# Keys and values of the given memory, projected beside the matrix memory instead of ahead of the cross-attention's queries

## The reference

```python
h = rmsnorm(x, norm_mix_g)
p = h @ w_in                      # queries, keys, values, gates of all branches
attn_out = sliding_window_attention(aq, ak, av, attn_sinks, slopes)
m_h = mlstm_chunkwise(mq, mk, mv, gif[..., :H], gif[..., H:])   # 4 heads of 128
x = x + concatenate([attn_out, sigmoid(mo) * m_h]) @ w_out

hm = rmsnorm(mem, norm_mem_g)     # mem: 256 rows of 1024, an input
kv = hm @ wkv                     # 1024 x 2048: keys, then values
q = rmsnorm(x, norm_xattn_g) @ wq
a = softmax(q k^T / 16)           # 4 heads of 256, 1024 x 256 scores each
x = x + (a v) @ wo
```

## Time and profile before

| what | value |
|---|---|
| time, median of 3 runs | 2593.92 us (2593.26 to 2597.9) |
| time of the profiled execution | 2593.7 us, its span 2591.9 |
| mean granted TensorE clock | 0.964 |
| TensorE busy (PE) | 2443.2 us, 94% of the span |
| VectorE busy (DVE) | 1407.1 us, 54% |
| ScalarE busy (ACT) | 932.0 us, 36% |
| GpSimd busy (POOL) | 78.3 us, 3% |

### The profile page before, as it was taken

How to read it: one execution, slowest core, us unless ns; L and a number is a source line. 1 busy time by engine, 2 the same in 40 slices (tenths; PEclk the granted TensorE clock), 3 DMA queues, 4 the chain that set the end, 5 groups by cost and what they waited for, 6 DMA issues and landing times.

```text
span 2591.9 us, 41445 instructions
## 1 busy us (share of the span) xinstructions
PE 2443.2 (94%) x17958; PEld 1969.8 (76%) x17958; DVE 1407.1 (54%) x2515; ACT 932.0 (36%) x1565; POOL 78.3 (3%) x61
## 2 busy tenths in 40 slices
PE   6999988999999999999999999899999996789879
PEld 5777756788888888888888888677777875577757
DVE  4584855655435555543555555563444455766653
ACT  3445432444333333422333423443232232334341
POOL 0000000000000000000000000020000001100000
PEclk9999977999999999999999999899999998799989
DMA  6453310434112333333333343333212312011043
GB/s 192 123 147 107 83 32 1 155 107 137 56 50 87 97 95 96 96 96 101 95 96 96 94 128 96 107 95 125 67 58 67 104 57 106 6 41 41 10 138 115
DMA packets 359310, 233.06 MB, mean 90 GB/s; under 512 B 9556, under 2 KB 332244, under 8 KB 359000
## 3 DMA queue, kind: packets, MB, share of 16 engines
q1 hardware_dynamic: 356392, 224.83, 29.0%
q10 hardware_dynamic: 2736, 5.57, 0.6%
HBM read 211.50 MB, written 18.87 MB: 89 GB/s over the span
## 4 chain that ended last, share of the span: by engine, by line
PE 87%; DVE 8%; ACT 2%; DMA 2%; issue 1%; POOL 0%; SPq 0%; ACTq 0%; DVEq 0%; POOLq 0%
PE PS L1325 21%; PE PS L1327 20%; PE PS L1326 20%; PE PS L1706 5%; PE PS L1311 3%; PE PS L1345 1%; PE PS L1347 1%; PE PS L1346 1%; PE PS L1624 1%; PE PS L1578 1%; PE PS L1553 1%; PE PS L1644 1%; PE PS L1609 1%; PE PS L1590 1%; DVE SR L1837 1%
## 5 line engine op out<-in xcount | busy, mean ns | idle before, releaser
L1325 PE MATMUL PS<-SR 128*128 128x512 f32 (+1 forms) x2400 | 955.9, 398 | 39.9 <-DVE SR L1837 35.0
L1326 PE MATMUL PS<-SR 128*128 128x512 f32 (+1 forms) x2400 | 933.7, 389 | 0.0
L1327 PE MATMUL PS<-SR 128*128 128x512 f32 (+1 forms) x2400 | 933.4, 389 | 0.0
L1837 DVE TENSOR_TENSOR SR<-SB,SR 128x1024 fp32r<-128x1024 f32 (+1 forms) x328 | 396.7, 1211 | 393.3 <-ACT SR L2523 392.9
L1325 PEld LDWEIGHTS PS<-SR 128*128 128x128 f32 x2400 | 452.8, 189 | 156.3 <-DVE SR L1837 36.4
L1327 PEld LDWEIGHTS PS<-SR 128*128 128x128 f32 x2400 | 452.7, 189 | 95.9
L1326 PEld LDWEIGHTS PS<-SR 128*128 128x128 f32 x2400 | 453.2, 189 | 89.6 <-issue 1.9
L2523 ACT ACTIVATE SR<-SB 128x1024 fp32r<-128x1024 f32 (+1 forms) x328 | 338.8, 1036 | 277.3 <-DMA SB<-in_w_down 102.7
L1706 PEld LDWEIGHTS PS<-SB 64*64 64x64 f32 x4096 | 128.3, 136 | 40.6 <-issue 20.9
L1706 PE MATMUL PS<-SB 64*64 64x64 f32 x4096 | 141.0, 222 | 12.4 <-DVE SB L2403 5.9
L1311 PE MATMUL PS<-SB 128*128 128x128 f32 (+2 forms) x688 | 107.7, 293 | 28.0 <-DVE SB L2285 15.0
(11 more groups left out here) (261 smaller groups left out, 2463.7 us busy)
## 6 DMA issues: line engine op xcount, KB each, us to landing
SB<-in_w_in SPq DMA_DIRECT2D x110, 512.0 KB, 4.0
SB<-in_w_up SPq DMA_DIRECT2D x88, 512.0 KB, 3.9
SB<-in_w_out SPq DMA_DIRECT2D x32, 512.0 KB, 4.5
SB<-in_w_down SPq DMA_DIRECT2D x32, 512.0 KB, 4.2
SB<-in_w_ada SPq DMA_DIRECT2D x12, 1024.0 KB, 6.3
asides<-SB SPq DMA_DIRECT2D x40, 256.0 KB, 3.5
SB<-in_wkv SPq DMA_DIRECT2D x16, 512.0 KB, 4.0
SB<-in_wq SPq DMA_DIRECT2D x16, 512.0 KB, 4.2
```

What stands on the lines that cost most here:

```text
L1325: pe.matmul(out, whi[:, k - k0, :], hi[k], start=(k == 0), stop=False)
L1326: pe.matmul(out, whi[:, k - k0, :], lo[k], start=False, stop=False)
L1327: i = pe.matmul(out, wlo[:, k - k0, :], hi[k], start=False, stop=(k == j.K - 1))
L1837: v.tensor_tensor(m.f32r(a, kn * cn), m.f32(a, kn * cn), m.f32r(a + 1024, kn * cn).bitcast(F32), SUB).then_inc(*on("split.v", p))
```

## The change

`mem` is loaded into X0 + 6144, a part of x's place, by a new step `mem_load` that stands at `mark("g")`, behind mv1, ahead of the load of the reset mask. Its norm is a side of the first flow behind the gates; kx, vx0 and vx1 are the last jobs of the first flow's main chain, and wait for the norm. Keys go to `kxs` in the second half of x's place, in-place of `mem`, values to two places `vxs`. `x_again` copies the keys by a DMA within SBUF (1 MB, `kmove`) to their final place, loads six of eight tiles of x's first half, copies a half of the values (0.5 MB, `vmove`), waits for `kmove`, and loads the rest of x. The jobs and units that read these places wait for the new semaphores instead of the old ones. `memory()` is gone.

```diff
-        self.memT = [work(28672 + 256 * k, 256) for k in range(8)]
-        self.qx, self.kx, self.vx = v3(work(16384, 8192), 8), v3(work(24576, 2048), 8), v3(work(26624, 2048), 2)
-        self.Pv2, self.PTv2 = [work(28672, 1024), work(29696, 1024)], [work(30720, 1024), work(31744, 1024)]
+        self.memT = [f32(X0 + 6144 + 256 * k, 256) for k in range(8)]
+        self.kxs, self.vxs = v3(f32(X0 + 6144, 2048), 8), [work(a, 1024) for a in (7168, 30752)]
+        self.qx, self.kx, self.vx = v3(work(16384, 8192), 8), v3(work(28672, 2048), 8), [work(a, 1024) for a in (31776, 30752)]
+        self.Pv2, self.PTv2 = [work(24576, 1024), work(25600, 1024)], [work(26624, 1024), work(27648, 1024)]
...
-        self.HM = self.parts(W0 + 30720, W0 + 28672, 256)
+        self.HM = self.parts(X0, X0 + 3072, 256)
...
         job(f"out{h}", d["w_out"], 0, 128, 8, m.MX[h], lambda k, h=h: [("mix.v", "lo", h, k)], "add", "gemm.v",
-            cut=4, dst=lambda t, h=h: m.xs[h][t], wait=lambda t, h=h: [(f"xr{h}", 0)], half=h)
+            cut=4, dst=lambda t, h=h: m.xs[h][t], wait=lambda t, h=h: [("xa0", 0), (f"xr{h}", 0)] if not h and t > 5 else [("xr1" if h else "xa0", 0)], half=h)
...
-    job("kx", d["wkv"], 0, 128, 8, m.HM, normed("mem"), "copy", "gemm.a", N=256, dst=lambda t: m.kx[:, t, :],
-        wait=UP("pe", "kv0"))
+    job("kx", d["wkv"], 0, 128, 8, m.HM, normed("mem"), "copy", "gemm.a", N=256, dst=lambda t: m.kxs[:, t, :],
+        wait=[("rms.v", "o", "mem", 7)])
...
-        "mem": Norm(m.memT, lambda k: [("mem", 0)], col("g_mem"), m.HM, st(273, 2), mldone, T=256),
+        "mem": Norm(m.memT, lambda k: [("mem", 0)], col("g_mem"), m.HM, st(273, 2),
+                    [("gates.pe", "t")], T=256),
...
-                        self.flagged("g", ("mark", "g"))),
+                        self.flagged("g", ("mark", "g"), ("mem_load",)),
+                        self.after("mem"), T("kx"), N("vx0"), N("vx1")),
...
-                  self.mlstm(0, 2), self.mlstm(1, 3))
+                  self.mlstm(0, 2), self.mlstm(1, 3),
+                  chain(self.after("gates"), self.rms("mem", self.room)))
...
-        self.flow(chain(T("out0"), self.after("parts"), T("out1"), self.flagged("kv0", ("mark", "kv0")), self.after("mem"),
-                        self.memory(), self.after("x0"), T("q0"), self.flagged("q0", ("mark", "q0")), self.after("x1"), T("q1"),
+        self.flow(chain(T("out0"), self.after("parts"), T("out1"), self.flagged("kv0", ("mark", "kv0")),
+                        self.opened_x(), self.after("x0"), T("q0"), self.flagged("q0", ("mark", "q0")), self.after("x1"), T("q1"),
...
+    def mem_load():
+        for e in S.upto("pe", "g"):
+            w.wait_ge(*e)
+        sp.dma_start(v3(m.f32(X0 + 6144, 2048), 8), d["memT"].rearrange("(k p) n -> p k n", p=128)).then_inc(*on("mem", 0, by=16))
+
     def x_again():
+
         mlstm_done()
-        for h in range(2):
-            sp.dma_start(m.XT[:, :, 512 * h:512 * h + 512],
-                         d["xT"][:, 512 * h:512 * h + 512].rearrange("(k p) n -> p k n", p=128)).then_inc(*on(f"xr{h}", 0, by=16))
-            if not h:
-                sp.dma_start(v3(m.work(28672, 2048), 8), d["memT"].rearrange("(k p) n -> p k n", p=128)).then_inc(
-                    *on("mem", 0, by=16))
+
+        def tokens(h, k0, k1):
+            return sp.dma_start(m.XT[:, k0:k1, 512 * h:512 * h + 512],
+                                d["xT"][128 * k0:128 * k1, 512 * h:512 * h + 512].rearrange("(k p) n -> p k n", p=128))
+        sp.dma_start(m.work(28672, 2048), m.f32(X0 + 6144, 2048)).then_inc(*on("kmove", 0, by=16))
+        tokens(0, 0, 6).then_inc(*on("xa0", 0, by=16))
+        sp.dma_start(m.vx[0], m.vxs[0]).then_inc(*on("vmove", 0, by=16))
+        w.wait_ge(*at("kmove", 0))
+        tokens(0, 6, 8).then_inc(*on("xr0", 0, by=16))
+        tokens(1, 0, 8).then_inc(*on("xr1", 0, by=16))
```

More of the change, by code:

```diff
@@ L907, in cross @@
             yield from self.after(("cs", n - 1))
-        yield from self.after("kv", f"q{n // 4}")
+        yield from self.after(f"q{n // 4}")
         yield from self.room((self.pairs, 1), (self.P, 1))
@@ L936, in crosses, with opened_x @@
             yield from self.cross(units.pop(0))
+    def opened_x(self):
+        for i in range(2):
+            self.P.give(i, ("upto", "pe", "kv0"))
+            self.PT.give(i, ("upto", "pe", "kv0"))
+        yield []
     def mix_later(self):
@@ L942, in mix_later @@
         yield [("mark", "parts")]
-    def memory(self):
-        yield from self.gemmT("kx")
-        for c in range(2):
-            yield from self.gemmN(f"vx{c}")
-        yield [("mark", "kv")]
-        kv = ("upto", "pe", "kv")
-        for i in range(2):
-            self.P.give(i, kv)
-            self.PT.give(i, kv)
-        self.done.add("kv")
     def ffn(self, half):
@@ L1570, in cross_o @@
         w.wait_ge(*at("cross.v", "pt", n))
+        w.wait_ge(*at("vmove", 0))
         for c in range(2):
```

13 lines of the change are left out of this document (8 added, 5 removed).

## The result

The changed kernel takes 2603.88 us, median of 11 executions (2602.32 to 2611.26), against 2594.2 us (2592.74 to 2602.9) before. The ratio is 1.0038, 95% interval 1.0027 to 1.0049: 9.7 us slower. The forecast was 2594.5 with a range up to 2603.0. In the experiments both kernels ran again: over all executions the changed one had a median of 2606.1 (22 executions), the kernel before 2595.3 (124); the means are 2605.9 and 2597.0.

What follows compares the result with a forecast made beforehand. TensorE, with 87% of the chain of waits, was taken as the bound. Terms 1.5 + 2.1 + 47.2 - 2.3 - 48.8 + 0.9 gave +0.6 on 2593.9, so 2594.5 us, no change that can be told; range 2584 to 2603.

Steps and rivals of the forecast that it cites:

- term 6: Copies back and reload of x, up to out0: w_out's fourth piece comes later behind 6 MB, net +0.9 us.
- term 4: Rest of the first pair of heads and the second pair, which starts staggered: -2.3 us, ends -11 and +1.
- nothing moves behind q0: From q0's start on, TensorE is 100% busy in either order, so no time changes there: 0 us.
- Term 1: Gates: the reset mask queues behind the 1 MB of `mem`, so the scan L2113 starts late, +1.5 us.
- Term 2: First pair's head part: the second head's transposes wait for the first head's 8 scalings because of the norm, +2.1 us.
- Term 3: Projections kx and vx among the first pair's steps: their TensorE time counts in full, +47.2 us, ends 44.2 and 49.5.
- coupled-queues rival: Steps among the projections: VectorE's in-order work holds splits 2.24 us at each of 4 steps; +9.6, 2603.5 us, chance 0.12.
- clock rival: Second pair of heads: products among the head parts keep the clock at 2.4 GHz; -8.1, 2585.8 us, chance 0.26.
- Late copies: At out0: copies within the chip take twice a load's time, delaying w_out's fourth piece; +7.2, 2601.1 us, chance 0.13.
- Term 5: Projection's old place ahead of q0: it falls away there, -48.8 us.

Runs made afterwards that it cites:

- mask_first: The changed kernel with the 16 KB reset mask loaded ahead of `mem` instead of behind it; 2600.35 us, ratio 1.0019 to the kernel before.
- after: The changed kernel in full, as first measured and profiled against the kernel before; 2603.88 us, ratio 1.0038.
- full pair: The first profiles of the kernel before and the changed kernel, neither shortened; medians 2594.2 and 2603.88 us.
- piece_first_cut: The changed kernel ended behind o1, with the load of x's second half put behind w_out's sixth piece; 861.70 us against 869.06 without that.

## Why the prediction was wrong

The forecast called no change that can be told; 9.7 us were lost, about 6 of them in the first block. The step that failed is term 6, and behind it term 4 and the claim that nothing moves behind q0.

- **What bounds the kernel** was read rightly: the projection counted in full in its new place, and q0 had no wait at its start.
- **Term 1** held: +1.4 to +1.8 for the mask by TensorE's wait (forecast 1.5), although its bounds, 350.5 to 351.8, hold 0.3 us more than 345.2 and the two transfer times give. The Trainium skill's sentence in "DMA: Bandwidth & Descriptors", on queues, rings and completion order, which was weighed there, agrees with mask_first: the mask waited only when it stood behind `mem`.
- **Term 2** came out right by luck: +1.7 to +2.1 against 2.1. It was to be a wait alone, the norm's products cancelling against out0. The wait grew by 1.2 us only (0.53 and 1.07 in after, 0.44 before); the rest is the norm's six products, about 1.3 us, which indeed left out0. So that much more of out0's and out1's +1.7 to +4.0 belongs to term 6. No run took the norm's place in the order apart.
- **Term 3** was a little high. By the full pair, from the first step to vx1's end, 56.17 us against 10.43 for the same steps before: +45.7 where 47.2 stood. In the three of the nine profiles without half clock at kx it is +43.9. TensorE did not wait for the norm's last part at kx, and none of the holds of the coupled-queues rival came: no wait for L1837 in kx or vx at all.
- **Term 4** failed by 4.7 us in that pair: 54.24 against 51.87, +2.4 instead of -2.3. The gain of 2.3 was put on the second pair losing its lockstep and on steps set among other products. At the old order's clock (17 us of half clock) the new order took 51.0, 0.8 us less and not 2.3; the other 3.2 us are 7 us more of half clock. The term's upper end, +1, allowed for less than that. The clock rival (2.4 GHz through the second pair) did not happen in any profile: 0.87 was the highest of the stretch.
- **Term 6** is the largest error: 0.9 stood for what the pairs show as 1.7 to 4.0 for the whole of out0 and out1, and piece_first_cut as 7.4 for the piece alone (the whole is less, since the norm's products and the old order's own wait of 0.9 to 2.8 us went). Three parts of it were too small. The piece came 21.1 to 21.8 us behind the first issue, not 19.7, since the new queue ran slower than 5.5 MB in 18.1 us. TensorE was at the fourth tile 18.1 us behind out0's start, not 19.6. And the half-clock stretch at the wait was in the rival alone, not in the sum, though the earlier trace rows had shown one behind the like wait.
- **The rivals.** "Late copies", 2601.1, named this place, but its mechanism was wrong, since a copy costs about what a load costs. "Coupled queues", 2603.5, came within 0.4 us of the measured time by luck: none of its holds happened.
- **Term 5** was read from one execution, in which the old place had the 2.24 us wait and a half-clock stretch behind it. All seven profiles of the old order have that wait, but only three the half clock: 48.8 to 48.9 us with it, 47.6 without. The base was itself an execution with a late q0: 608.9, against 606.2 to 609.0 in the other profiles of that order without added products.
- **"Behind q0 nothing should move"** holds for the order and for TensorE's idle time (95 to 96 us behind that point in all six profiles), not for the time. The range, 2584 to 2603, was made of the first block's uncertainties alone. The 1740 us behind it differ by 14 us between the six profiles. The range's upper end lay 0.9 us below the measured median.

## What to carry to other kernels

When work moves to an earlier place, price what else its data needs on the queues there and at the place it is read. Here the move itself won some 5 us in three profiles and 2 us or nothing in six, while the mask (1.6), the norm (about 2, not taken apart) and a weight piece behind 5.5 MB of other transfers (7.4) cost more than that. A transfer that isn't due for 50 us (x's second half) should not stand ahead of one that is due in 18. Where a stage's clock varies, compare its parts at equal half-clock time before blaming their order. And where a kernel has a long unchanged part whose clock varies, end the kernel early to measure the changed one: four executions of each then told 6 us apart, where eleven of the whole gave 9.7 us within 2.8, first block and tail in one number.

## What the runs showed of the hardware

- A plain copy from SBUF to SBUF of 1 MB took 5.4 us from issue to landing with other transfers behind it (the first row below, of after), and 6 MB with two such copies took 21.1 to 21.8 us until w_out's fourth piece landed, with loads in their place 21.1. No gain over loads from HBM showed.

```profile
SB<-SB SPq DMA_DIRECT2D x1, 1024.0 KB, 5.4
...
SB<-SB SPq DMA_DIRECT2D x1, 512.0 KB, 10.4
```

- TensorE's granted clock in identical work differs from execution to execution: 113 to 143 us at 1.2 GHz behind 1000 us in six profiles of the two full kernels, and 14 us of time with it; 113 to 127 in the three of the kernel before. A shift of the work by 2.96 us left the median within the noise of the repeated kernel.
- The same wait is not always followed by the same clock. At out0's fourth tile the clock was at 1.2 GHz for 6.8 us with waits of 3.69, 4.15, 4.42, 4.47 and 4.80 us, for 3.4 us with waits of 2.52 to 3.24 us and of 3.71 us (mask_first), and not at all with waits of 0.93 to 1.35 us. Behind the wait of 2.24 us in the old place it fell for 3.4 us in three profiles and stayed at 2.4 GHz in four. The old order's wait at out0's fourth tile itself measured between 0.93 and 2.78 us.
- TensorE can be busy without a gap at 1.2 GHz: from 424.2 to 437.9 in the profile of before it was busy 13.70 of 13.7 us (selections, scores, transposes) with a granted clock of 0.50, and all seven profiles of the old order have this stretch of 13.6 to 13.7 us.
